# Forget-gate decode of batches 0 to 3 inside chunk compression, one tile per step

## The chip, the cores and the metric

The kernel runs on one core of a Trainium2 chip. The number is the device time of one execution in microseconds (us). Engines are named as in the profile: PE is TensorE's matmul, PEld its weight load, DVE is VectorE, ACT is ScalarE, POOL is GpSimd and SP is SyncE; the last two, and sometimes ACT, issue transfers. They run their own programs and meet at semaphores.

## What is computed

One layer of a hybrid decoder for a prompt of 256 tokens and for 8 decoding sequences ("batches") of 4 tokens each, over a paged cache of 2048 rows per sequence. Two mixers run side by side. NSA has 8 query heads over 2 key heads and three branches: attention over compressed blocks, over 16 selected blocks, over a window. FoX (the forget-gate mixer) has 8 heads and full softmax attention, with sums of log forget gates added to the logits. A gated merge and a convolutional FFN follow. Cut to what the change touches:

```python
def compress_rows(rows, pe, w1, b1, w2):            # once for keys, once for values
    chunks = rows.reshape(B, nc, 16, 2, 64)
    lo = einsum('bcpgd,pdh->bcgh', chunks + pe[:16], w1[:16])
    hi = einsum('bcpgd,pdh->bcgh', chunks + pe[16:], w1[16:])
    return einsum('bcgh,he->bcge', gelu(lo[:, :-1] + hi[:, 1:] + b1), w2)

def fox_attend(q, cq, segs):                        # segs: the cache, then the new rows
    logits = [einsum('bthd,bshd->bhts', q, k) * scale + cq - ck for k, v, ck in segs]
    pr = masked_softmax(concat(logits))
    return sum(einsum('bhts,bshd->bthd', pr_part, v) ...)
```

The FoX cache is 4 MB of keys and 4 MB of values per sequence, 64 MB in all; the compressed NSA caches are 16 MB, the selected ones 16 MB.

## The kernel before

The program is a row of stages (tokens, projection, prompt attention, compression, decode, merge, FFN), each a block in which every engine has its own list of instructions in an order written by hand. Two stages matter.

**Compression** (`stage_compress`, from line 1028; 177.4 to 337.8 in the profile). Sixteen tiles of 1 MB (8 for keys, 8 for values) are gathered into four raw buffers by POOL (`gather`, L1006). The work has `NSTEP` = 32 steps; four steps make a group of two tiles, four groups the keys and four the values. In step k, `fill` (L1143) turns an eighth of two raw tiles by 8 PE transposes into two PSUM banks; pairs of banks alternate, 0 and 1, 2 and 3, and a fill runs two steps ahead. `evacuate` copies the banks to a rounded high part on ACT (L246) and the rest to a low part on DVE (L251). `hidden` (L1166) takes 48 products of these with the high and low parts of the first-layer weights `w1`, in banks 4 and 5. Those parts are made a quarter at a time by `weights` (ACT, then DVE) in steps 0 to 3 for the keys and in steps 12 to 15 for the values. `gelu` (L1257) follows each group, `outputs` a step later through bank 6, and bank 7 serves the norm of the compressed keys and the prompt's attention over chunks. The raw `w1` of the values is loaded in one go (SP, L1014) over that of the keys, once these are split (`w_low` at 4).

**Decode** (`stage_decode`, 337.8 to 577.2). Tiles of 1 MB come through a ring of `DEC_RING` = 8 buffers, gathered by POOL (L1461) as each buffer is freed, 84 in all. Batches 0 to 3 are half 0, batches 4 to 7 half 1. A half of FoX has 16 key tiles: `turn_keys` (L1627) makes 16 transposes into four banks of four, ACT (L1874) and DVE (L1855) copy them out by turns, `key_products` (L1738) takes 4 products of 512 columns into bank 4; every fourth tile adds the forget bias (L1736) and is taken by DVE (L1955). ACT takes the exponentials (L1880), PE turns the probabilities (L1636). Then 16 value tiles (`fox_values`, L1806), 4 products each; after four of them DVE copies the sums out of bank 6 (`take_slots`, L2072) and PE folds them (L1811) in bank 7. NSA of the same half runs between: scores, a selection by DVE in six parts (`select`), its key and value tiles, a merge. `decode_steps` is the hand-written list of all these steps, and `decode_order` puts the turning of one step ahead of the products of the one before; PE, ACT and DVE all walk this one list, each in its order. At the end of the stage the gate weights of the merge are split and multiplied (`split`, `gates`).

## Time and profile before

| | |
|---|---|
| time, median of 3 runs | 930.11 us (929.46 to 933.62) |
| span of the profiled execution | 930.0 us |
| PE busy | 864.0 us, 93% |
| DVE, ACT, POOL busy | 513.4, 378.5, 160.9 us |
| DMA | 191.89 MB, mean 206 GB/s |

The span runs from the first to the last instruction of the profiled execution, and that execution has no time of its own in the results; its span lies 0.1 us from the median of the runs, so that next to nothing lies around it. Busy time of an engine is the time in which at least one of its instructions was running. A matmul's record includes the way through the array, so records overlap; the pace of a run of them is read from the starts, and a busy PE isn't one at its peak. "Idle before" is the time in which an engine had nothing before an instruction, with what ended it. PEclk is the granted clock of TensorE as a share of 2.4 GHz.

### The profile page before, as it was taken

To read this page: it belongs to the slowest core of one execution; us is meant where nothing else is said; L and a number is where in the kernel's file an instruction comes from. 1 tells how busy PE (TensorE), PEld (TensorE's weight loads), DVE (VectorE), ACT (ScalarE), POOL (GpSimd) and SP (SyncE) were. 2 spreads that over 40 slices of the span, in tenths; PEclk is the share of its full clock that TensorE was granted. 3 is DMA by queue.
4 is the path that set the end of the run, shared out by engine and by line. 5 is a ranking of instruction groups with operands and counts; after the bars stand their busy time and mean duration, and the time that the engine had idled before them with its cause. 6 is when DMAs were issued, how large, how long until landed. Compare 5 with 4: busy or idle time off the path is not lost. (4 is left out here: it accounts for less than half of the span.)

```text
span 930.0 us, 18007 instructions
## 1 busy us (share of the span) xinstructions
PE 864.0 (93%) x7191; PEld 708.9 (76%) x7191; DVE 513.4 (55%) x941; ACT 378.5 (41%) x704; POOL 160.9 (17%) x262
## 2 busy tenths in 40 slices
PE   4999788799999999999998977999979999999997
PEld 3888678689889977655655455998679998998985
DVE  5466567433434566754367434465656565565654
ACT  4346575542424323453224422443244443444432
POOL 2000041211121022333434511000001010010100
PEclk8999989999999899999999999999979999999999
DMA  6542195164424269989999994966054544555412
GB/s 218 164 162 87 25 319 221 56 156 136 162 94 182 92 262 385 327 325 418 418 416 420 382 409 121 297 216 223 9 175 149 175 136 135 165 199 177 135 45 61
DMA packets 90640, 191.89 MB, mean 206 GB/s; under 512 B 7466, under 2 KB 68682, under 8 KB 78186
## 3 DMA queue, kind: packets, MB, share of 16 engines
q0 software_dynamic: 15408, 106.04, 29.5%
q1 hardware_dynamic: 74876, 83.91, 29.1%
q8 instruction: 49, 0.80, 0.4%
q10 hardware_dynamic: 288, 0.97, 0.3%
q14 instruction: 19, 0.16, 0.0%
HBM read 187.44 MB, written 7.64 MB: 210 GB/s over the span
## 5 line engine op out<-in xcount | busy, mean ns | idle before, releaser
L1627 PEld LDWEIGHTS banks<-consts_base,stream_rows 128*128 128x128 f32 x672 | 73.4, 142 | 32.7 <-issue 27.3
L1874 ACT ACTIVATE keys_turned<-banks 128x512 f32<-128x512 f32 x94 | 54.9, 596 | 102.1 <-PE banks L1627 97.3
L258 PE MATMUL banks<-tokens_turned_high,w_gates_high 128*128 128x288 f32 x288 | 86.4, 300 | 3.5 <-PEq L191 2.3
L1627 PE MATMUL banks<-consts_base,stream_rows 128*128 128x128 f32 x672 | 83.1, 276 | 6.2 <-DVE fox_probs_turned L1865 2.6
L259 PE MATMUL banks<-tokens_turned_low,w_gates_high 128*128 128x288 f32 x288 | 85.4, 297 | 0.0
L1166 PE MATMUL banks<-chunks_turned_high,cmp_w_high 64*128 64x256 f32 (+1 forms) x512 | 79.6, 303 | 5.3 <-DVE cmp_w_low L251 2.7
L260 PE MATMUL banks<-tokens_turned_high,w_gates_low 128*128 128x288 f32 x272 | 81.7, 300 | 0.0
L1166 PE MATMUL banks<-chunks_turned_low,cmp_w_high 64*128 64x256 f32 (+1 forms) x512 | 76.3, 290 | 0.0
L1166 PE MATMUL banks<-chunks_turned_high,cmp_w_low 64*128 64x256 f32 (+1 forms) x512 | 76.3, 289 | 0.0
L251 DVE TENSOR_TENSOR chunks_turned_low<-banks,chunks_turned_high 128x512 fp32r<-128x512 f32 x64 | 41.1, 684 | 48.0 <-ACT chunks_turned_high L246 48.0
L1855 DVE COPY keys_turned<-banks 128x512 f32<-128x512 f32 x74 | 50.2, 690 | 28.1 <-PE banks L1627 23.1
L246 ACT ACTIVATE chunks_turned_high<-banks 128x512 fp32r<-128x512 f32 x64 | 34.7, 595 | 74.6 <-PE banks L1143 74.6
L1166 PEld LDWEIGHTS banks<-chunks_turned_high,cmp_w_high 64*128 64x128 f32 x512 | 51.9, 194 | 12.7 <-issue 9.3
L258 PEld LDWEIGHTS banks<-tokens_turned_high,w_gates_high 128*128 128x128 f32 x288 | 55.2, 192 | 6.0 <-issue 3.5
L258 PE MATMUL banks<-tokens_turned_high,w_up_gate_high 128*128 128x288 f32 x192 | 58.0, 302 | 0.0
L260 PE MATMUL banks<-tokens_turned_high,w_up_gate_low 128*128 128x288 f32 x192 | 57.1, 297 | 0.0
L259 PE MATMUL banks<-tokens_turned_low,w_up_gate_high 128*128 128x288 f32 x192 | 56.7, 295 | 0.0
L259 PEld LDWEIGHTS banks<-tokens_turned_low,w_gates_high 128*128 128x128 f32 x288 | 55.6, 193 | 0.4
L1166 PEld LDWEIGHTS banks<-chunks_turned_high,cmp_w_low 64*128 64x128 f32 x512 | 52.4, 194 | 0.1
L1166 PEld LDWEIGHTS banks<-chunks_turned_low,cmp_w_high 64*128 64x128 f32 x512 | 52.1, 194 | 0.0
L260 PEld LDWEIGHTS banks<-tokens_turned_high,w_gates_low 128*128 128x128 f32 x272 | 52.0, 191 | 0.0
L2692 POOL COPY conv_new_state<-up_turned 128x2 f32 (+1 forms) x24 | 16.4, 681 | 200.4 <-ACT up_turned L2658 200.4
(451 smaller groups left out, 2107.0 us busy)
## 6 DMA issues: line engine op xcount, KB each, us to landing
w_up_gate<-in_w_up SPq DMA_DIRECT2D x12, 1024.0 KB, 7.3
w_up_gate<-in_w_gate SPq DMA_DIRECT2D x12, 1024.0 KB, 9.8
w_down<-in_w_down SPq DMA_DIRECT2D x12, 1024.0 KB, 5.1
w_in_slot<-in_w_in SPq DMA_DIRECT2D x7, 1424.0 KB, 6.2
w_gates<-in_w_in SPq DMA_DIRECT2D x10, 512.0 KB, 7.3
cmp_w<-in_cmp_w_k SPq DMA_DIRECT2D x4, 512.0 KB
cmp_w<-in_cmp_w_v SPq DMA_DIRECT2D x4, 512.0 KB
stream_rows<-in_state_win_k SPq DMA_DIRECT2D x8, 256.0 KB
```

What stands on the lines that cost most here:

```text
L246: return nc.scalar.activation(high, x, ACT.Copy)
L251: return nc.vector.tensor_tensor(low, x, high.bitcast(F32), ALU.subtract)
L258: nc.tensor.matmul(out, lh, rh, start=start, stop=False, **kw)
L259: nc.tensor.matmul(out, lh, rl, start=False, stop=False, **kw)
L260: return nc.tensor.matmul(out, ll, rh, start=False, stop=stop, **kw)
L1166: ins = nc.tensor.matmul(c.ps[4 + g][:, 0:w], x[rows, half * CS + 4 * q + i, :], y[k % 2][rows, i, src], start=(q + i + half + part == 0), ...
L1627: ins = nc.tensor.transpose(bank(t)[:, q * P:(q + 1) * P], src, ident)
L1855: copy(kT[kbuf[step]][:, x, :], bank(t)).then_inc(copied[e], 1)
L1874: copy = lambda a, b: nc.scalar.activation(a, b, ACT.Copy)
L2692: nc.gpsimd.tensor_copy(dst[:, :, 0:2], ue[f][:, SEQ:SEQ + 2].unsqueeze(1))
```

## The change

FoX of half 0 leaves decode and is done in compression. Steps 0 to 15 take one key tile each (`key_at`), steps 18 to 30 one value tile, two in steps 20, 23 and 26 (`value_at`); steps 16 and 17 turn the probabilities. Two new buffers take the tiles by turns (`gather_fox`): one in the region where the low weights stood, one beside the raw weights. For that, the low parts of `w1` are written over the raw ones (`cmp_w1_low` at the address of `cmp_w1`), the raw value weights come in quarters, each after the last use of its keys' quarter (`load_w1_late`), and they are split in steps 14 to 17. PSUM banks 2 and 3 go to the new work, so fills have only banks 0 and 1 and run one step ahead; bank 7 sums the new logits and values, and what used bank 7 uses bank 2. `hidden` is called in two halves with the turning of two blocks of a key tile before each. The sums of log forget gates move from decode to steps 1 to 3. Decode keeps NSA of both halves and FoX of half 1, in a new order. The turned prompt keys stand apart from the sample's (`kT_prompt`, `fkT_prompt`), so that their place can be used for the turned key tiles. `outputs` of the FoX rows of half 0 are made at the end of compression.

The core of the diff:

```diff
             for m in range(NB):
                 pool.wait_ge(qk, m + 1)
                 chunks.gather(m)
+            chunks.gather_fox(0)
...
+    def load_w1_late(self, sp, q):
+
+        for g in range(NG):
+            for half in range(2):
+                rows = slice(half * CS + 4 * q, half * CS + 4 * q + 4)
+                sp.dma_start(self.w1[g * HD:(g + 1) * HD, rows, :], self.c.d["cmp_w1_v"][0].rearrange("s e h -> e s h")[:, rows, :]).then_inc(self.load_late[q], 16)
...
+    key_at = {k: k for k in range(NU)}
+    early = (20, 23, 26)
+    value_at, n = {}, 0
+    for k in range(NU + 2, NSTEP - 1):
+        m = 2 if k in early else 1
+        value_at[k] = tuple(range(n, n + m))
+        n += m
...
-        bank = lambda k, x: c.ps[2 * (k % 2) + x]
+        bank = lambda k, x: c.ps[x]
+        copied_probs = {1: (1, 33), 2: (0, 33), 3: (1, 34), 4: (0, 34), 0: (0, 35)}
+        bank_of_probs = {1: 3, 2: 2, 3: 3, 4: 2, 0: 7}
         @block.sync
         def _(sp):
+            c.load_fox(sp)
             load_consts(sp)
-            c.load_fox(sp)
-            sp.wait_ge(w_low, 4)
-            chunks.load_w1(sp, 1)
+            for q in range(4):
+                sp.wait_ge(used, 4 * (NGR - 1) + q + 1)
+                chunks.load_w1_late(sp, q)
...
+            def fox_rows(n):
+                if n < NU + 2:
+                    pool.wait_ge(f_turned, 4 * (n - 2) + 4)
+                else:
+                    pool.wait_ge(f_values, n - 2 - NU + 1)
+                chunks.gather_fox(n)
...
+            def turn_keys(u, x):
+                t = 4 * u + x
+                if x == 0:
+                    pe.wait_ge(chunks.fox_in[u % 2], 16 * (u // 2 + 1))
+                if t >= 2:
+                    pe.wait_ge(f_copied[x % 2], t // 2)
+                for q in range(4):
+                    ins = nc.tensor.transpose(c.ps[2 + x % 2][:, q * P:(q + 1) * P], tiles[u % 2][:, q, x * P:(x + 1) * P], c.k("ident"))
+                ins.then_inc(f_turned, 1)
...
+            def new_values():
+                pe.wait_ge(f_copied[0], copied_probs[0][1])
+                pe.wait_ge(f_copied[1], copied_probs[3][1])
...
             fill(0)
-            fill(1)
             for k in range(NSTEP):
                 G, q = divmod(k, 4)
-                hidden(k)
-                if k + 2 < NSTEP:
-                    fill(k + 2)
+                values_now, unit = value_at.get(k, ()), key_at.get(k)
+                if k + 1 < NSTEP:
+                    fill(k + 1)
+                if unit is not None:
+                    turn_keys(unit, 0)
+                    turn_keys(unit, 1)
+                if k == 4:
+                    new_keys()
+                if k == NU + 2:
+                    new_values()
+                if values_now:
+                    values(values_now[0])
+                hidden(k, 0)
+                if unit is not None:
+                    turn_keys(unit, 2)
+                    turn_keys(unit, 3)
+                if values_now and values_now[0] % 4 == 3:
+                    fold_slots(values_now[0] // 4)
+                hidden(k, 1)
+                if unit is not None:
+                    key_products(unit)
+                if k == 1:
+                    logf_sums()
+                if k == NU:
+                    turn_probs(1)
+                    turn_probs(2)
+                if k == NU + 1:
+                    turn_probs(3)
+                    turn_probs(4)
+                    turn_probs(0)
...
+                for i in values_now[1:]:
+                    values(i)
+                    if i % 4 == 3:
+                        fold_slots(i // 4)
...
             outputs(NT - 1)
+            pe.wait_ge(f_out, 1)
+            for q in range(4):
+                ins = nc.tensor.transpose(c.ps[7][:, q * P:(q + 1) * P], fo[:, q * P:(q + 1) * P], c.k("ident"))
...  (ACT, in step k)
                 if k + 1 < NSTEP:
                     evacuate(k + 1)
+                if unit is not None:
+                    fox_keys(unit, 1)
+                if k == NU:
+                    soften(1)
+                    soften(2)
+                if k == NU + 1:
+                    fox_probs(1, 1)
+                    soften(3)
+                    soften(4)
+                    soften(0)
+                if k == NU + 2:
+                    fox_probs(3, 3)
                 if G == 0 and q < 3:
                     weights(0, q + 1)
-                if G == NGR - 1:
-                    weights(1, q)
+                if 0 <= k - (4 * NGR - 2) < 4:
+                    weights(1, k - (4 * NGR - 2))
+                if unit is not None:
+                    fox_keys(unit, 3)
...  (DVE, in step k)
+                if unit is not None:
+                    fox_keys(unit, 0)
                 if k + 1 < NSTEP:
                     evacuate(k + 1)
+                if k == 2:
+                    logf_rows()
+                if k == 3:
+                    cum_rows()
+                if 0 <= k - (4 * NGR - 2) < 4:
+                    weights(1, k - (4 * NGR - 2))
+                if unit is not None:
+                    fox_keys(unit, 2)
+                if k == NU + 1:
+                    fox_probs(2, 2)
+                if k == NU + 2:
+                    fox_probs(4, 4)
+                    fox_probs(0, 5)
...  (the order of decode, new)
+    start = (fox(1, 0) + [("sums", "both", 0, 0)] + fox(1, 1, 2) + rows + fox(1, 3, 4) + new("nsa", 0) + new("fox", 1) + fox(1, 5) + exps("cmp", 0, 0)
+             + fox(1, 6) + norm(0) + fox(1, 7) + score(0) + fox(1, 8) + select(0, 0) + fox(1, 9) + select(0, 1) + nsa(0, 0) + select(0, 2) + fox(1, 10)
+             + select(0, 3) + exps("win", 0, 0) + select(0, 4) + fox(1, 11) + select(0, 5) + fox(1, 12) + nsa(0, 1, 2) + fox(1, 13) + nsa(0, 3) + fox(1, 14)
+             + nsa(0, 4) + fox(1, 15) + nsa_probs(0, 0, 1) + exps("sel", 0, 0, 1) + nsa_probs(0, 2) + exps("fox", 1, 1, 2) + exps("sel", 0, 2, 3, 4)
+             + exps("fox", 1, 3, 4, 0) + nsa_probs(0, 3, 4))
+    middle = (probs(1, 1, 2) + nsa_probs(0, 5, 6) + probs(1, 3, 4) + vals(1, 0) + nsa_probs(0, 7) + probs(1, 0) + vals(1, 1) + nsa_vals(0, 0) + vals(1, 2) + nsa_vals(0, 1)
+              + vals(1, 3) + nsa_vals(0, 2) + fold("fox", 1, 0) + vals(1, 4) + nsa_vals(0, 3) + vals(1, 5) + fold("nsa", 0, 0) + merge("nsa", 0) + vals(1, 6) + new("nsa", 1)
+              + out("nsa", 0) + vals(1, 7) + exps("cmp", 1, 0) + fold("fox", 1, 1) + norm(1) + vals(1, 8) + score(1) + select(1, 0) + vals(1, 9) + select(1, 1) + nsa(1, 0)
+              + select(1, 2) + vals(1, 10) + select(1, 3) + exps("win", 1, 0) + select(1, 4) + vals(1, 11) + select(1, 5) + fold("fox", 1, 2))
+    end = (nsa(1, 1, 2, 3) + vals(1, 12) + nsa(1, 4) + nsa_probs(1, 0, 1) + vals(1, 13) + exps("sel", 1, 0, 1, 2) + nsa_probs(1, 2) + exps("sel", 1, 3, 4)
+           + nsa_probs(1, 3, 4, 5, 6, 7) + branch(0) + vals(1, 14) + nsa_vals(1, 0) + branch(1)
+           + split(0) + branch(2) + nsa_vals(1, 1) + branch(3) + vals(1, 15) + nsa_vals(1, 2) + gates(0, 0) + nsa_vals(1, 3) + fold("nsa", 1, 0) + fold("fox", 1, 3) + merge("nsa", 1)
+           + merge("fox", 1) + gates(0, 1) + out("nsa", 1) + split(1) + out("fox", 1) + gates(1, 0) + split(2) + gates(1, 1))
```

## Rows read from the trace of the kernel before

**Rows 1.** The page, its first part: busy us of each engine and instructions.
```profile
PE 864.0 (93%) x7191; PEld 708.9 (76%) x7191; DVE 513.4 (55%) x941; ACT 378.5 (41%) x704; POOL 160.9 (17%) x262
```

**Rows 2.** Busy time by window: compression, decode, and the middle of decode.
```profile
core 0: us, PE busy (x) PEld busy (x) DVE busy (x) ACT busy (x) POOL busy (x), PEclk, DMA share, GB/s
177.40:337.80 160.40, 153.44 (x1888) 140.11 (x1889) 70.50 (x118) 56.69 (x95) 25.46 (x41) 0.96 0.43 140
337.80:577.20 239.40, 220.34 (x2080) 140.50 (x2081) 130.74 (x281) 86.54 (x164) 78.54 (x81) 0.99 0.93 364
...
420.00:560.00 140.00, 127.09 (x1290) 78.20 (x1286) 68.06 (x146) 45.12 (x88) 51.14 (x53) 0.98 1.01 409
```

**Rows 3.** PE's timeline in decode: start, us, engine, line, operation, count.
```profile
361.41 1.97 PE L1627 MATMUL banks<-consts_base,stream_rows 128*128 128x128 f32 x16
363.31 1.07 PE L1738 MATMUL banks<-keys_turned,fox_q_decode 128*32 128x512 f32 x8
364.31 1.97 PE L1627 MATMUL banks<-consts_base,stream_rows 128*128 128x128 f32 x16
...
419.13 1.06 PE L1806 MATMUL banks<-stream_rows,fox_probs_turned 128*32 128x512 f32 x8
420.02 1.04 PE L1738 MATMUL banks<-keys_turned,fox_q_decode 128*32 128x512 f32 x8
```

**Rows 4.** PE's timeline, waits: in brackets the idle time before, and its releaser.
```profile
203.38 0.39 PE L1166 MATMUL banks<-chunks_turned_high,cmp_w_high 64*128 64x256 f32 x2 [1.47 <-ACT cmp_hidden L1257]
...
505.56 1.09 PE L1627 MATMUL banks<-consts_base,stream_rows 128*128 128x128 f32 x4 [2.29 <-DVE fox_probs_turned L1865]
...
540.57 0.27 PE L1772 MATMUL banks<-sample_rows_kept,nsa_probs_turned 128*32 128x128 f32 x1 [2.12 <-DMA stream_rows<-in_cache_sel_v,eighth_row]
...
543.05 1.06 PE L1806 MATMUL banks<-stream_rows,fox_probs_turned 128*32 128x512 f32 x8 [0.65 <-DMA stream_rows<-in_cache_fox_v,fox_row]
546.52 0.35 PE L1772 MATMUL banks<-sample_rows_kept,nsa_probs_turned 128*32 128x128 f32 x1 [2.40 <-DMA stream_rows<-in_cache_sel_v,eighth_row]
```

**Rows 5.** PE's timeline in a compression step: the fill, the first products, the next fill.
```profile
206.45 1.09 PE L1143 MATMUL banks<-consts_base,stream_rows 128*128 128x128 f32 x8
207.47 0.39 PE L1166 MATMUL banks<-chunks_turned_high,cmp_w_high 64*128 64x256 f32 x2
...
210.54 1.09 PE L1143 MATMUL banks<-consts_base,stream_rows 128*128 128x128 f32 x8
```

**Rows 6.** Groups by line, ACT in compression: count | busy us, mean ns | idle before.
```profile
L246 ACT ACTIVATE chunks_turned_high<-banks 128x512 fp32r<-128x512 f32 x64 | 34.7, 595 | 74.6 <-PE banks L1143 74.6
L246 ACT ACTIVATE cmp_w_high<-cmp_w 128x1024 fp32r<-128x1024 f32 x8 | 8.5, 1061 | 9.0 <-PE banks L1166 9.0
...
L1257 ACT ACT_TABLE_LOAD x3 | 3.8, 1283 | 2.4 <-DVE cmp_bias L1330 2.4
```

**Rows 7.** Groups by line, DVE in compression.
```profile
L251 DVE TENSOR_TENSOR chunks_turned_low<-banks,chunks_turned_high 128x512 fp32r<-128x512 f32 x64 | 41.1, 684 | 48.0 <-ACT chunks_turned_high L246 48.0
L251 DVE TENSOR_TENSOR cmp_w_low<-cmp_w,cmp_w_high 128x1024 fp32r<-128x1024 f32 x8 | 9.8, 1225 | 8.3 <-ACT cmp_w_high L246 7.8
```

**Rows 8.** Timeline of DVE and ACT in decode.
```profile
471.81 1.46 DVE L2087 COPY nsa_sample_out_turned<-banks 64x16 f32<-64x16 f32 x8
...
487.21 1.09 DVE L1997 TENSOR_TENSOR block_compared<-block_scores 128x900 f32<-128x900 f32 x1
...
496.26 0.71 ACT L1880 ACTIVATE fox_logits<-fox_logits,fox_negmax 128x512 f32<-128x512 f32 x1
...
539.33 2.29 DVE L251 TENSOR_TENSOR w_gates_low_early<-w_gates_early,w_gates_high_early 128x2048 fp32r<-128x2048 f32 x1 [1.11 <-ACT w_gates_high_early L246]
```

**Rows 9.** DMA issues from 186 to 340: count, median us from issue to landing.
```profile
stream_rows<-in_cache_cmp_v,eighth_row POOLq DMA_INDIRECT x8, 8.4
```

**Rows 10.** Busy time by window, columns as in rows 2: two stretches at a lower clock.
```profile
506.00:509.00 3.00, 3.00 (x16) 1.50 (x18) 0.98 (x5) 0.60 (x1) 2.08 (x3) 0.50 1.02 426
...
182.00:188.00 6.00, 5.94 (x49) 5.72 (x50) 2.13 (x3) 0.46 (x1) 0.02 (x1) 0.50 0.01 3
```

**Rows 11.** POOL's timeline: the gather of an nsa value tile.
```profile
525.03 1.01 POOL L1461 DMA_INDIRECT stream_rows<-in_cache_sel_v,eighth_row  x1 [0.30 <-issue]
```

457 lines of the change are left out of this document (309 added, 148 removed).

## Prediction

> **What bounds the kernel now.** I read the totals first [rows 1]: PE is busy for 93% of the span, 66 us are left, and that is all that a rearrangement of equal work can win. Then the windows by stage [rows 2]. Chunk compression (177.4 to 337.8) has 6.96 us without a matmul (160.40 - 153.44) at 140 GB/s; decode (337.8 to 577.2) has 19.06 us (239.40 - 220.34) at 364 GB/s, and from 420 to 560 it moves 409 GB/s with the DMA share at 1.01. So the reader sees two claims to the bound in decode, PE and DMA. The third view, PE's timeline, says which ends last: a forget-gate key tile is 16 transposes and 4 products that start at 361.41, 363.31 and 364.31, 2.90 us one behind the other without a gap, and a value tile takes 0.89 us (419.13 to 420.02) [rows 3]. A pair of tiles is 3.8 us of PE for 2.1 MB, 552 GB/s: above what the DMA gives, but the keys alone want only 362. Of decode's 19.06 us of idle PE, a transfer ended 5.17 (2.12 + 0.65 + 2.40) [rows 4]; the rest waited for a DVE or ACT that was busy elsewhere, as in the 2.29 us before 505.56, or lay in short gaps. The DMA is full, yet mostly behind PE. What bounds is PE, in its program order.
>
> **The work that moves.** 16 key tiles and 16 value tiles leave decode: 16 x 2.90 + 16 x 0.89 = 60.6 us, and with the bias products, the folds, the new keys and values and the turned probabilities (none changed in number or shape) some 74 us. The same instructions are added to compression, so this term is zero in the sum, whatever its size, as long as PE's pace is the same in both places.
>
> **Compression, what is new on PE.** A step of it is now one fill of 8 transposes, 1.02 us (206.45 to 207.47), and 48 products of `hidden`, 3.07 us (to 210.54) [rows 5]. The change cuts `hidden` in two with transposes between. The first pair of a run costs more than the steady pace: the 24 pairs at 0.12 us would be 2.86, so a run has 0.21 us at its ends, 16 more of them: **+3.4 us**. A key step then lasts 1.0 + 0.95 + 1.64 + 0.95 + 1.64 + 1.0, about 7.1 us. I laid each engine's queue beside it, with 0.60 us for a 128x512 copy on ACT and 0.68 on DVE, and 1.06 (ACT) and 1.23 (DVE) for a quarter of the weights [rows 6, 7]. In most key steps everything is ready: `evacuate` ends at 3.6, the last key copies at 4.7 (DVE) and 5.1 (ACT), the products want them at 5.9. The single pair of fill banks costs nothing then, because the fill is asked for a whole step later. The cover fails in five places:
> - Step 2: DVE has `logf_rows` (three operations of 128x512 or its like, 1.9 by the row of 0.68), then a weight quarter, then the third key copy, at 7.5 instead of 6.4: **1.1**.
> - Step 16: two exponentials (0.71 each [rows 8]) come behind a table load of 1.28 [rows 6]: **0.4**.
> - Step 17: ACT does evacuate, a probability copy, three exponentials and only then the last quarter of the v weights (ends 5.7); DVE waits for that, splits it (6.9), and copies piece 2 (7.6). PE has stood before the turn of piece 4, which needs that bank, since 4.7: **3.0**.
> - Step 18: `new_values` stands behind only a fill, but wants pieces 4 and 0, which DVE copies after `evacuate(19)`: ready at 4.1, wanted at 1.0: **3.1**.
> - Steps 20, 23, 26: the second value tile of the step is followed at once by its fold, which waits for a 0.68 copy and two semaphores: 3 x 0.95 = **2.9**.
>
> At the end DVE has the merge (0.6 + 0.75) and four sums more behind the last product: **1.5**. Given back: the two waits for the hidden rows (1.47 at 203.38 [rows 4] and its like in the other half, 1.1), since key work now lies before them: **-2.6**. Sum of the stalls 9.4 us. ACT's queue otherwise has room. POOL's: each gather costs it about 1.0 and stands behind the tail of the next group, which waits for `used`; it is still two steps ahead. SP's: the v weights are issued by quarters as `hidden` frees them, 10 us before ACT wants them. For a gather in compression the nearest row is 8.4 us to landing for two issued together [rows 9]; the window from release to use is 2 x 5.1 - 1 = 9.2 us in value steps and 10 in key steps. I take nothing for it.
>
> **Decode.** Its 19.06 us of idle fall by the 5.17 of transfers: 32 of 84 ring tiles are gone, so 54.5 MB remain, 133 us at 409 GB/s, against about 145 us of PE. But the same keys that left were the cover for the selection of the other half. In the new order:
> - End of `start`: ACT has ten exponentials in a row (6 us and more) before it copies turned piece 3 of the nsa probabilities, whose bank piece 5 wants: **3.4**, where before key tiles lay between.
> - `new`, `out` (eight copies, 1.46 us), `take_slots`, then a fold with one value tile (0.89) as cover: **2.9**. Then three steps of `select` (1.09 each), a window maximum and the slot copy before the next fold: **3.7**. Waiting for the nsa merge: **0.5** [rows 8].
> - `end`: the split of gate weights (2.29 on DVE, after ACT's half of it [rows 8]) stands before the slot copy that nsa_vals(1,2) needs: **3.0**. `out` nsa and the next split before gates(1,0), with half a microsecond of PE as cover: **3.7**. Smaller: **1.3**.
> - Kept: 0.7 in the keys, 2.3 at the stage's end.
>
> Together 21.5, **+2.4** against 19.06.
>
> **The clock.** After the 2.29 us without a matmul at 503 the granted clock was 0.50 for 506 to 509, and at the first `hidden`, which waits for its weights, it was 0.50 for 182 to 188 [rows 10]: the lower of its two levels, 1.2 GHz. An episode of 3.4 to 6.8 us by those rows costs half of that in PE work. The two stages have waits of 2.3 us or more about five times now and I count nine after. Four more at 1.7 would be 7; as PE at half pace also shortens the waits behind it, I take **+4**. Bounds: 0 (the waits break up) and +13.
>
> **A rule that speaks the other way.** The row first: in decode LDWEIGHTS are busy 140.50 of 239.40 us, 59%, under a DMA share of 0.93 [rows 2]. The Trainium skill, Perfetto Trace Analysis, "Identifying the Most-Contended Engine", says that matmul busy time is no measure of how near PE is to its limit and that LDWEIGHTS and the DMA are to be compared; its "Optimization Strategy" advises mixing stages with different limits, and that is this change. By it decode would shrink with its bytes and compression would swallow the tiles. I go by the gapless timeline [rows 3] for the forecast, and give the rule its own case.
>
> **The sum.** 930.0 (the span; the median of the runs is 930.11, so both stand for each other) + 3.4 + 9.4 + 2.4 + 4 = **949**.
>
> **Rivals.**
> - *Relief of the DMA.* The mechanism in this kernel: most idle of decode is really late data in small portions, and it goes with the bytes. 930 - 13 (two thirds of 19.06) - 2.6 + 3.4 + half of the new waits in compression (6) = **924**. For it: 1.01 share for 140 us. Against: only 5.17 us have a transfer as releaser.
> - *A draw.* The waits of DVE's order overlap each other more than I reckon, so half of the 12 and half of the 21.5 appear: 930 + 3.4 + 3.4 + (11 - 19) + 2 = **932**.
> - *The gathers become the wait.* Two buffers instead of eight. With the ring full a tile was issued at 525.03 and its value products began at 540.57 [rows 4, 11], 15.5 us; if, beside the 512 KB quarters and the chunk pairs, one takes 2 us more than its window in eight steps, that is 16 us: **965**. It decides from a landing of 9.2 us after release.
>
> **How the numbers follow.** Forecast 0.60, relief 0.15, draw 0.12, gathers 0.13. The forecast's own range, from clock at 0 and stalls at two thirds to clock at +13, is 940 to 960. The range reaches to the draw and to the gathers, 928 to 965. About 0.5%, 4.6 us, is what a measurement of this kernel can tell from no change. Faster: the relief, 0.15. Same: the draw, 0.12. Slower: the forecast and the gathers, 0.73.
>
> **What would show it.** Right: compression 240 to 260 us long, with PE idle before the turn of piece 4 and before `new_values` and released by DVE; decode 165 to 175 us, no PE wait ended by a transfer, its waits ended by slot copies and splits; more stretches at 0.50. Wrong: decode under 155 us (relief), or key steps in compression with PE waiting for `fox_rows_early` (gathers), or a key step far from 7.1 us, which would mean that PE's pace isn't the same there.

## The result, and the profile after

The changed kernel takes 975.71 us (median of 4 runs, 972.41 to 978.46), the kernel before 929.79 beside it: a ratio of 1.051, 95% interval 1.0473 to 1.0547, **45.9 us slower**. The forecast was 949, 19 us slower, with a range up to 965. The direction was right, the size was not, and the time lies outside the range.

The totals, and the two stages by window (columns as in rows 2):

```profile
PE 880.1 (91%) x7191; PEld 713.9 (74%) x7191; DVE 513.2 (53%) x941; ACT 380.0 (39%) x706; POOL 159.6 (16%) x262
```

```profile
core 0: us, PE busy (x) PEld busy (x) DVE busy (x) ACT busy (x) POOL busy (x), PEclk, DMA share, GB/s
178.60:442.05 263.45, 239.86 (x2511) 183.60 (x2511) 105.71 (x191) 81.44 (x141) 53.60 (x72) 0.94 0.60 209
442.05:618.70 176.65, 150.06 (x1457) 102.12 (x1458) 95.51 (x208) 63.17 (x120) 48.44 (x49) 0.95 0.81 303
540.00:560.00 20.00, 13.09 (x101) 6.31 (x93) 11.73 (x31) 2.71 (x5) 6.60 (x7) 0.91 1.02 395
```

The same 7191 matmuls are busy 16.1 us longer than before [rows 1]. The two stages lasted 160.40 + 239.40 = 399.8 us [rows 2] and last 263.45 + 176.65 = 440.1: all of the 40.4 us between the two spans lies in them (the stages ahead are 1.2 longer, those behind 1.1 shorter). Idle PE in them was 6.96 + 19.06 = 26.0 and is 23.6 + 26.6 = 50.2, 24.2 more; the other 16.1 are matmuls that take longer. So there are two accounts to settle, where PE waits and why its work is slower; the forecast had 11.8 for the first (9.4 + 2.4) and 7.4 for the second (3.4 + 4).

The difference of the medians is 5.5 us more than that of the two spans. 3.3 of it is that the profiled execution of the changed kernel (972.41) is the fastest of its four. The rest lies on the side of before: its span of 930.0 is 2 us longer than goes with its median of 929.79, as 1.7 to 2.4 us lie outside the span in the executions whose time and span are both on record. (The record doesn't say which time belongs to that span; the first listed, 933.62, is likely.) Part of this is the clock: the four executions of the changed kernel have a mean granted clock of 0.964, 0.959, 0.955 and 0.960, the profiled one the highest, and that of before has 0.972, where all executions of before beside the experiments, on other chips, have 0.973 to 0.987. So what the spans below give to the clock is rather too little for the medians.

Where PE waits in compression: its timeline, with the idle time and its releaser in brackets.

```profile
322.49 0.63 PE L1326 MATMUL banks<-consts_fox,fox_logits_early 128*128 128x128 f32 x4 [3.48 <-DVE fox_logits_early L1577]
...
329.74 1.90 PE L1336 MATMUL banks<-sample_rows_kept,fox_new_logits_early 128*32 128x512 f32 x8 [2.87 <-DVE fox_new_logits_early L1577]
...
371.37 1.93 PE L1348 MATMUL banks<-fox_rows_early,fox_logits_early 128*32 128x512 f32 x8 [2.75 <-DMA fox_rows_early<-in_cache_fox_v,fox_row]
...
432.36 0.66 PE L1425 MATMUL banks<-consts_base,fox_rows_out_early 128*128 128x128 f32 x4 [0.39 <-DVE fox_rows_out_early L1590]
442.09 3.22 PE L1953 MATMUL banks<-consts_base,stream_rows 128*128 128x128 f32 x14 [9.07 <-PEq L191]
```

The first two are the turn of piece 4 and `new_values`, as forecast. The third is a tile that came late. The fourth line is PE's last work of the stage and the fifth the first of decode: 9.07 us with the barrier (L191) as releaser, where before there were 1.66:

```profile
337.81 1.94 PE L1627 MATMUL banks<-consts_base,stream_rows 128*128 128x128 f32 x16 [1.66 <-PEq L191]
```

DVE's last sums began at 433.39 and took 1.27; behind them nobody computes. POOL had this:

```profile
430.16 0.94 POOL L1790 DMA_INDIRECT stream_rows<-in_cache_fox_k,fox_row  x1 [7.30 <-PE banks L1244]
431.40 0.93 POOL L1790 DMA_INDIRECT stream_rows<-in_cache_fox_k,fox_row  x1 [0.30 <-issue]
442.71 0.93 POOL L1790 DMA_INDIRECT stream_rows<-in_cache_fox_k,fox_row  x1 [10.38 <-POOLq L191]
```

Ring tiles 4 and 5 are gathered last, behind the final product of `hidden` (the change made them wait for `used` at its end, as their place is freed then), and the barrier's drains (L191) stand at 441.3, 9.0 us behind the last gather. Ahead of them every engine has a drain of its own at the end of its list (L188), and POOL's is long: first in the changed kernel, then in the kernel before, with ns of duration and the start.

```profile
L188 POOLq DRAIN  x1: 11151/11151/11151, 429.9 to 429.9; - x1
...
L188 POOLq DRAIN  x1: 9994/9994/9994, 326.0 to 326.0; - x1
```

It ends at 441.1, 2.0 us behind the landing of the last gather (7.6 us after its issue at 431.40). In before it ended at 336.0, 8.5 us behind the last gather of the stage (issued at 327.51) and 0.9 us ahead of DVE's.

And in decode:

```profile
520.60 1.65 PE L1979 MATMUL banks<-consts_base,sel_logits 128*128 128x128 f32 x8 [2.66 <-ACT nsa_probs_turned L2191]
...
546.39 0.62 PE L2130 MATMUL banks<-fox_slot_sums,consts_base 128*32 128x512 f32 x1 [2.90 <-DVE fox_slot_sums L2368]
...
552.36 3.28 PE L1953 MATMUL banks<-consts_base,stream_rows 128*128 128x128 f32 x16 [2.39 <-DMA stream_rows<-in_state_win_k]
...
562.36 1.92 PE L2130 MATMUL banks<-fox_slot_sums,consts_base 128*32 128x512 f32 x2 [3.02 <-DVE fox_slot_sums L2368]
...
593.67 0.27 PE L2093 MATMUL banks<-sample_rows_kept,nsa_probs_turned 128*32 128x128 f32 x1 [2.58 <-DVE nsa_slot_sums L2339]
...
608.68 0.40 PE L264 MATMUL banks<-tokens_turned_high,w_gates_high 128*128 128x288 f32 x1 [3.45 <-DVE w_gates_low_in_place L257]
```

Five of the six were forecast by name, with sizes up to 0.7 us above these. The third was not: window keys that landed late, in a stretch where the DMA share is 1.02 at 395 GB/s and PE is busy for 13.09 of 20 us (the last window above).

### The profile page after: what moved, and what is told of

Its sections match the earlier page's. It is cut to its first block and busy times, and to the rows that moved or that the text cites. A ratio compares the mean times of both kernels' runs of the same rounds, so it can differ in the third digit from the quotient of the medians.

```text
span 970.4 us, 18010 instructions
## 1 busy us (share of the span) xinstructions
PE 880.1 (91%) x7191; PEld 713.9 (74%) x7191; DVE 513.2 (53%) x941; ACT 380.0 (39%) x706; POOL 159.6 (16%) x262
## 5 line engine op out<-in xcount | busy, mean ns | idle before, releaser
L1244 PE MATMUL banks<-chunks_turned_low,cmp_w_high 64*128 64x256 f32 (+1 forms) x512 | 73.8, 283 | 0.0
L1244 PE MATMUL banks<-chunks_turned_high,cmp_w_low 64*128 64x256 f32 (+1 forms) x512 | 73.7, 283 | 0.0
L1953 PEld LDWEIGHTS banks<-consts_base,stream_rows 128*128 128x128 f32 x416 | 48.6, 148 | 32.0 <-issue 28.7
L1953 PE MATMUL banks<-consts_base,stream_rows 128*128 128x128 f32 x416 | 54.3, 287 | 13.2 <-PEq L191 9.1
L1244 PEld LDWEIGHTS banks<-chunks_turned_high,cmp_w_high 64*128 64x128 f32 x512 | 49.3, 188 | 19.9 <-issue 17.3
L2191 ACT ACTIVATE keys_turned<-banks 128x512 f32<-128x512 f32 x62 | 35.8, 596 | 68.1 <-PE banks L1953 68.0
L1244 PEld LDWEIGHTS banks<-chunks_turned_low,cmp_w_high 64*128 64x128 f32 x512 | 49.5, 189 | 0.0
L1244 PEld LDWEIGHTS banks<-chunks_turned_high,cmp_w_low 64*128 64x128 f32 x512 | 49.3, 188 | 0.0
L1524 DVE COPY fox_keys_early<-banks 128x512 f32<-128x512 f32 x32 | 22.1, 690 | 46.3 <-PE banks L1292 43.0
```

The source lines that it names most:

```text
L1244: ins = nc.tensor.matmul(c.ps[4 + g][:, 0:w], wt[rows, half * CS + 4 * q + i, :], y[k % 2][rows, i, src], start=(q + i + half + part == 0) ...
L1524: nc.vector.tensor_copy(kq[x][:, :], c.ps[2][:, :]).then_inc(f_copied[0], 1)
L1953: ins = nc.tensor.transpose(bank(t)[:, q * P:(q + 1) * P], src, ident)
L2191: copy = lambda a, b: nc.scalar.activation(a, b, ACT.Copy)
```

## Experiments

Each kernel was timed beside the kernel before on its chip, which gave 926.6 to 927.8 us there; the changed kernel at its ratio of 1.051 would be about 975 beside it. Differences under about 5 us between two changed kernels are inside the intervals. Stage lengths and waits are those of one profiled execution each.

**Late gathers out of compression (e1).** Two gathers cross a stage boundary:

```
-            for n in range(6):
-                if n < 4:
-                    pool.wait_ge(turned, NSTEP - 4 if n < 2 else NSTEP)
-                else:
-                    pool.wait_ge(used, NSTEP)
+            for n in range(4):
+                pool.wait_ge(turned, NSTEP - 4 if n < 2 else NSTEP)
                 gather_decode_rows(c, n)
...
-            for n in range(6, len(ring)):
+            for n in range(4, len(ring)):
```

> The changed kernel, but the gathers of ring tiles 4 and 5, which stood behind the last product of hidden at the end of compression, are POOL's first two of decode instead. In the changed kernel PE stood still for 9.07 us before decode, and every engine's drain lay 8.9 us behind POOL's last gather (431.40 + 0.94 to 441.3). Theory A (the stage can't end until POOL's last gathers have landed): that wait falls to the 1 to 2 us of before, the 10.2 us at half clock behind it is gone too, decode's later tiles come no later; 975.7 - 7.4 - 1.8 = about 966, between 963 and 969. Theory B (the boundary waits for something else, DVE's sums or the barrier itself): time within 2 us of 975.7 and the wait still about 9 us. If tiles 4 and 5 come too late for PE in decode, a wait ended by a transfer of stream_rows shows before 460 and gives back 2 to 5 us.

Measured: 967.27 us, ratio 1.0432 (1.0391 to 1.0472), 7.2 us of the 9.2 expected. The first rows of decode, on PE and on POOL:

```profile
433.17 3.39 PE L1950 MATMUL banks<-consts_base,stream_rows 128*128 128x128 f32 x16 [2.91 <-PEq L191]
```

```profile
419.16 0.94 POOL L1787 DMA_INDIRECT stream_rows<-in_cache_fox_k,fox_row  x1 [0.30 <-issue]
433.79 0.94 POOL L1787 DMA_INDIRECT stream_rows<-in_cache_fox_k,fox_row  x1 [13.69 <-POOLq L191]
```

The wait fell from 9.07 to 2.91, and no tile came late at decode's start (later there are 5.7 us of waits for data, against 3.2). So the two late gathers held the stage open (theory A). POOL's own drain now ends at 428.9, again 2.0 us behind the landing of its last gather (426.9), and that is no longer last: the barrier's drains at 432.4 stand behind DVE's four sums (430.64 + 1.27 and their latency). The 2.91 us are the 1.66 of before and 1.25 more, near the 1.5 for the stage's end which the forecast had.

```profile
L188 POOLq DRAIN  x1: 11202/11202/11202, 417.7 to 417.7; - x1
```

**DVE's and ACT's order (e2).** The copies of the turned probabilities first, and a fold that followed its value tile at once moved into the next step:

```
+                if k == NU + 1:
+                    fox_probs(2, 2)
+                if k == NU + 2:
+                    fox_probs(4, 4)
+                    fox_probs(0, 5)
                 if k + 1 < NSTEP:
                     evacuate(k + 1)
...
+                while late:
+                    fold_slots(late.pop())
                 hidden(k, 1)
...
                     values(i)
                     if i % 4 == 3:
-                        fold_slots(i // 4)
+                        late.append(i // 4)
```

> The changed kernel with two orders mended: in steps 17 and 18 DVE and ACT copy the turned probabilities first, ahead of the evacuation and the weight quarter; and the three folds that followed their value tile at once are done in the middle of the next step. In the changed kernel PE waited 3.48 us before the turn of piece 4, 2.87 before new_values and 0.81 + 0.80 + 0.81 before those folds, 8.8 together. Theory A (a wait of over about 2.4 us also costs a stretch at half clock behind it, 3.4 us long at 322.9 and at 329.7 in the profiled run): 8.8 - 0.5 that stays, and 3.4 for the clock, so 975.7 - 11.7 = about 964, between 962 and 967. Theory B (only the waits go): 975.7 - 8.3 = 967.4. Theory C (the waits of DVE are made up elsewhere in the same steps): less than 4 us, over 971.5.

Measured: 964.93, ratio 1.0398 (1.0353 to 1.0444), 10 us less: theory A by the forecast and by the trace, though the interval holds B's 967.4 too. The wait of 3.48 and the three of 0.8 are gone, 1.67 is left before `new_values`, and the granted clock is 1.00 from 322 to 352 where it was 0.72 from 322 to 334.

**Value gathers ahead of chunk gathers (e3).** POOL's order within a step:

```
-                if q == 2 and G + 2 < NT:
-                    pool.wait_ge(turned, 4 * G + 4)
-                    for b in range(2):
-                        chunks.gather(2 * (G + 2) + b)
                 for i in value_at.get(k, ()):
                     if i + 2 < NU:
                         fox_rows(NU + i + 2)
+                if q == 2 and G + 2 < NT:
+                    pool.wait_ge(turned, 4 * G + 4)
+                    for b in range(2):
+                        chunks.gather(2 * (G + 2) + b)
```

> The changed kernel with POOL's order in each third step of a group turned: the gathers of the forget-gate rows stand ahead of the two gathers of chunk rows, which nobody wants for five steps. In the changed kernel the value tile used at 371.37 was issued at 361.60, behind the chunk gathers of 359.12 and 360.36, and PE waited 2.75 us for it; 6.8 us at half clock followed. Theory A (the two chunk gathers, 2.1 MB, lie in front of it on the same queue): the wait is gone and with it the stretch at half clock, 975.7 - 2.75 - 3.4 = 969.5, between 968 and 973. Theory B (a landing simply takes longer than a step's window there): the wait stays within 1 us, time within 2 us of 975.7.

Measured: 971.54, ratio 1.0476 (1.044 to 1.0512), about 3 us less, inside what can't be told apart. The trace tells more: the tile at 371 came in time, and another was late instead, behind the same pair of chunk gathers:

```profile
363.14 0.93 POOL L1018 DMA_INDIRECT stream_rows<-in_cache_cmp_v,eighth_row  x1 [0.30 <-issue]
365.75 0.93 POOL L1027 DMA_INDIRECT fox_rows_early<-in_cache_fox_v,fox_row  x1 [1.68 <-PE banks L1348]
```

```profile
375.25 1.60 PE L1348 MATMUL banks<-fox_rows_early,fox_logits_early 128*32 128x512 f32 x8 [2.23 <-DMA fox_rows_early<-in_cache_fox_v,fox_row]
```

From 365.75 to 375.25 are 9.5 us. The rival of late gathers had put the line at 9.2. A tile of the same size with nothing in front of it landed 5.5 us after its issue (350.17, the same run).

**Quarter rows in compression (e7).** It leaves out three quarters of the rows of the forget-gate tiles gathered there:

```
+        w = P // 4 if n >= 2 else P
-        nc.gpsimd.indirect_dma_start(self.fox[n % 2][:, :], None, table, ...
+        nc.gpsimd.indirect_dma_start(self.fox[n % 2][0:w, :], None, table, ...
```

> The changed kernel, but the forget-gate gathers inside compression move 32 of 128 rows each (from the third on): 23 MB less in compression, the same instructions otherwise; what the other rows hold is left from the first tiles. It measures everything that gathering into two buffers costs there. Theory A (PE bounds compression, one gather of 32 comes late): the wait of 2.75 us at 371.37 and the 6.8 us at half clock behind it go, 975.7 - 6 = about 969.5, between 968 and 973. Theory B (the rival of the forecast: gathers are late in eight steps and more): 960 or less. Theory C (the DMA's load slows what else uses memory, so PE's pace in key steps falls with the bytes): key steps of 7.9 to 8.6 us become shorter by 0.3 or more.

Measured: 972.12, ratio 1.0489 (1.0445 to 1.0532). B is out: all the bytes of these tiles together are worth 2 us, 6 at most. But A had the wrong cause, as its wait stayed:

```profile
368.87 1.07 PE L1349 MATMUL banks<-fox_rows_early,fox_logits_early 128*32 128x512 f32 x8 [2.38 <-DMA fox_rows_early<-in_cache_fox_v,fox_row]
```

A tile of 0.26 MB, issued at 359.51, was as late as one of 1 MB. What it had in front of it was the pair of chunk gathers, unchanged (356.99 and 358.26). C is out too: all key steps behind the first last as long as in the changed kernel, to 0.01 us (8.06, 7.88, 8.45 and so on in both).

**The three together (e5).** e1, e2 and e3 in one kernel.

> The changed kernel with the three mendings together: late gathers moved into decode, DVE's and ACT's order in steps 17 and 18 with the folds in the next step, value gathers ahead of chunk gathers. Alone they gave 7.6, 10 and 3.4 us against the changed kernel at 1.051 times the kernel before. Theory A (they lie in different places and add up): ratio 1.051 - 0.0225 = 1.028, between 1.025 and 1.032, which is 26 us over the kernel before, and what the forecast left out is explained. Theory B (tiles that are asked for sooner meet a full DMA, and waits for transfers take the place of the others): 1.034 to 1.040, with more than 5 us of PE waits ended by transfers in the view of the waits.

Measured: 960.83, ratio 1.0359 (1.0317 to 1.0401): 14 us, not the 21 of the parts. That is theory B's range, though with four intervals in the comparison the 7 us are not clear of them. PE came sooner to a tile that had the pair in front of it:

```profile
353.44 0.93 POOL L1018 DMA_INDIRECT stream_rows<-in_cache_cmp_v,eighth_row  x1 [0.30 <-issue]
356.05 0.94 POOL L1027 DMA_INDIRECT fox_rows_early<-in_cache_fox_v,fox_row  x1 [1.68 <-PE banks L1345]
```

```profile
366.08 1.94 PE L1345 MATMUL banks<-fox_rows_early,fox_logits_early 128*32 128x512 f32 x8 [4.62 <-DMA fox_rows_early<-in_cache_fox_v,fox_row]
```

The waits ended by a transfer sum to 8.4 us in its two stages, 5.9 in the changed kernel; so theory B's sign of more than 5 us didn't tell the two apart. The stages tell more. Compression fell by 15.7 us (263.5 to 247.8), against 8.1, 10.5 and 3.5 in e1, e2 and e3, 22 together. Waits for value tiles there are 6.5 us against 2.7, which is 3.8 of the 6.4 that are missing: that much is theory B. Decode is 4.1 us longer (180.8 against 176.7) at the same idle PE (25.7 and 26.6), because its granted clock was 0.92 and not 0.95; in e1, e2 and e3 it lasted 179.5 to 179.9 at 0.92 to 0.93. What moves the clock there from one execution to the next isn't settled.

**The pair taken apart (e9).** e1 and e2, one chunk gather in each of two steps, behind the value gather, and two value tiles in steps 20, 24 and 28:

```
-    early = (20, 23, 26)
+    early = (20, 24, 28)
...
+                if q >= 2 and G + 2 < NT:
+                    pool.wait_ge(turned, 4 * G + 4)
+                    chunks.gather(2 * (G + 2) + q - 2)
```

> The mendings of e1 and e2 together, and the gathers of compression spread: the two gathers of chunk rows, which POOL issued one behind the other, in two steps, each behind the value gather of its step, and the steps with two value tiles moved from 20, 23, 26 to 20, 24, 28. In e5 a value tile issued at 356.05, behind the chunk pair of 352.20 and 353.44, ended a wait of 4.62 us at 366.08; with quarter rows (e7) the wait at that place was still 2.38 us, so it is the pair of 1 MB gathers in front of a tile, not the tiles' own bytes. Theory A (the pair in front is the cause): no PE wait over 1 us ended by fox_rows_early, no stretch at half clock at 365 to 373, so 960.8 - 4.6 - 1.6 - 3.4 = about 951, ratio 1.024 to 1.031 to the kernel before. Theory B (two buffers are too few however the gathers stand): waits of 3 us and more in all remain somewhere from 340 to 420 and the ratio is 1.033 or more.

Measured: 955.38, ratio 1.0275 (1.0234 to 1.0316), theory A in the main: PE's waits for these tiles in compression fell to

```profile
PE banks L1344 <- DMA fox_rows_early<-in_cache_fox_v,fox_row: 2.0, 2, 1.4
```

(total, count, longest), the longest still over the 1 us expected, and the stretch of 6.8 us at half clock there is 3.4 (at 371.7), though the expectation had none left. In decode, though, waits for transfers grew to 7.1 us: `fox_rows` 6.4 and window keys 0.7, against 3.2 in the changed kernel. That this comes of what was mended upstream is not shown: the same waits were 6.7 us in e3, whose decode and boundary are those of the changed kernel, and 1.9 in e5.

**Bytes taken out of decode of before (e4).** It leaves out three quarters of the rows of the forget-gate tiles of batches 0 to 3 there:

```
+    w = P // 4 if job == "fox" and half == 0 and n >= DEC_RING else P
-    c.nc.gpsimd.indirect_dma_start(c.stream[r][:, :], None, table, ...
+    c.nc.gpsimd.indirect_dma_start(c.stream[r][0:w, :], None, table, ...
```

> The kernel before, unchanged in order, but the gathers of the forget-gate tiles of batches 0 to 3 in decode (from the ninth ring tile on) move only 32 of 128 rows: about 19 MB less in decode; what the other rows hold is left from earlier tiles. It tells the largest gain that taking these bytes out of decode could bring. Theory A (PE bounds decode, the DMA is full behind it; the view of the forecast): only the waits that a transfer ended in the first half may go, and those of 540.57, 543.05 and 546.52 lie in the second half: 929.8 - 0 to 3, so 927 to 930. Theory B (the rival: two thirds of decode's 19 us of idle PE is late data): 929.8 - 8 to 13, so 917 to 922.

Measured: 925.33, ratio 0.9978 (0.9955 to 1.0): 2 us, 4 at most. In its profiled execution decode lasted 235.0 us against 239.4 (1.7 of these 4.4 are the clock), and transfers ended 4.2 us of waits against 5.17, with the DMA share down from 0.93 to 0.83. Theory A; the relief that rows 2 seem to offer (a share of 1.01 for 140 us) is not there to be had. The expectation calls it the largest gain, but it leaves out 19 MB of the 33.6 that the change moves, none from the first eight ring tiles.

**One value tile moved in decode (e8).**

```
-              ... + vals(1, 6) + new("nsa", 1)
-              + out("nsa", 0) + vals(1, 7) + exps("cmp", 1, 0) ...
+              ... + vals(1, 6) + vals(1, 7) + new("nsa", 1)
+              + out("nsa", 0) + exps("cmp", 1, 0) ...
```

> The changed kernel with one step of decode moved: the value tile vals(1,7) stands ahead of new(nsa,1) and out(nsa,0), so that DVE's slot copy of batch 5 comes ahead of the eight copies of out (1.46 us) and PE has new and out as cover before fold(1,1). In the changed kernel that fold waited 2.90 us at 546.39. Theory A (DVE's order is the cause, as the forecast has it): the wait falls under 1 us, with half of a 3.4 us stretch at half clock: 975.7 - 2.5 - 1.7 = about 971.5, between 970 and 973.5. Theory B (the DMA is full there, 395 GB/s from 540 to 560 at a share of 1.02, and PE only waits for the next tile instead): the wait for the fold goes and waits ended by stream_rows grow by as much; time within 2 us of 975.7.

Measured: 972.32, ratio 1.0485 (1.0446 to 1.0524): between the two theories, and inside what can't be told apart from no gain. The trace decides: the wait for the fold is gone, so DVE's order was its cause, and two others stand in its place, one for a tile and one for DVE again.

```profile
541.50 1.94 PE L2125 MATMUL banks<-stream_rows,fox_probs_turned 128*32 128x512 f32 x8 [1.69 <-DMA stream_rows<-in_cache_fox_v,fox_row]
550.00 0.46 PE L2043 MATMUL banks<-cmp_logits,consts_select 128*128 128x128 f32 x2 [2.53 <-DVE cmp_logits L2284]
```

1.69 + 2.53 is more than the 2.90 that went, while the 2.39 for the window keys fell to 0.36. So the wait for the fold was mended and others came; waits for data in decode were 2.5 us in all, against 3.2.

**PE kept busy in three waits (e6).** `spin(bank, n)` is n transposes of the identity into a free bank, which nobody reads:

```
+                    spin(6, 26)
                     turn_probs(4)
...
+                    spin(6, 20)
                     new_values()
...
             ins.then_inc(f_out_turned, 1)
+            spin(1, 68)
```

> The changed kernel with useless transposes of a constant on PE ahead of three of its waits: 26 before the turn of piece 4 (3.48 us), 20 before new_values (2.87), 68 before the end of compression (9.07), none of them longer than the wait that it fills, so the waits for DVE and for the drain end when they did. Theory A (the clock falls because PE stood still): the stretches at half clock that began at 322.9, 329.7 and 435.5 are gone, PE's work behind them takes 1.7 + 1.7 + 1.8 = 5.2 us less: about 970.5 against 975.7, and the granted clock of 322 to 334 and of 440 to 446 is 1.00. Theory B (it falls for the load of the whole chip or by a rhythm of its own): the same stretches at half clock, somewhere near, and a time within 2 us of 975.7.

Measured: 967.84, ratio 1.043 (1.0382 to 1.0478), 7 us less. The same stretches in both kernels, first the changed one (the column after POOL's count is the granted clock):

```profile
322.00:334.00 12.00, 8.63 (x45) 5.02 (x47) 2.92 (x7) 1.57 (x3) 2.28 (x3) 0.72 0.43 153
...
442.00:446.00 4.00, 3.91 (x20) 3.94 (x21) 1.47 (x3) 0.82 (x2) 1.86 (x2) 0.51 0.76 275
```

```profile
322.00:334.00 12.00, 10.87 (x112) 8.68 (x110) 3.73 (x8) 1.58 (x3) 4.76 (x4) 1.00 0.51 176
...
440.00:446.00 6.00, 6.00 (x53) 5.00 (x54) 3.48 (x7) 2.39 (x4) 3.62 (x4) 1.00 0.84 304
```

The three waits were ended by the same events (DVE's copies and POOL's drain don't depend on the fillers), and the three stretches at 0.50, the lower level of 1.2 GHz, are gone. So it was PE's standing still that they followed from, not a rhythm of the chip. In the changed kernel's two stages these stretches cost 23.8 us of PE work by the granted clock of each microsecond (3.3 of it inside the 9.07 us wait, where nothing was lost), against 10.2 in before: **+10.3**. (The short idle times inside the other stretches are still in it; by busy PE alone the difference is 9.5.)

**Fillers in the kernel before (e10, e12).** If the clock is worth that much, before should gain too.

```
+            spin(nc, c, 6, 17)
...
+            pe.wait_ge(z_out[1], NZC)
+            spin(nc, c, 4, 20)
...
+                    if n == 2:
+                        spin(nc, c, 6, 24)
...
+            spin(nc, c, 2, 12)
...
+                    spin(nc, c, 7, 21)
...
+            spin(nc, c, 7, 20)
...
+            spin(nc, c, 0, 24)
...
+            spin(nc, c, 0, 14)
```

> The kernel before with useless transposes of a constant on PE in eight of its waits, nothing else changed: 17, 20 (behind a wait for ACT's last copy of the bank that they write) and 12 at the ends of the first three stages, 24 and 21 ahead of the first wait of attention and of compression, 20 at the end of decode, 24 and 14 at the end of the merge; 0.12 us each, about as long as the waits or shorter. In the profiled run of before, half clock followed these waits at 17 to 25, 113 to 124, 181 to 189, 577 to 581 and 679 to 690, 18.7 us of PE time lost in all. Theory A (the clock falls because PE stood still, as e6 showed in the changed kernel): most of these stretches go, and the time falls by 8 to 17 us, to a ratio of 0.982 to 0.991. Theory B (the chip takes the clock back elsewhere, or the waits were what the clock needed): stretches at half clock appear in other places, ratio 0.996 to 1.003. If a filler outlasts its wait, up to 0.5 us is lost in each place.

Measured: 924.03, ratio 0.9962 (0.9944 to 0.998): a gain, but 3.5 us instead of 8 to 17. The first filler ran at half the pace and outlasted its wait:

```profile
15.34 3.89 PE L372 MATMUL banks<-consts_base 128*128 128x128 f32 x17
20.00 1.40 PE L515 MATMUL banks<-w_in_slot,sample_turned 128*32 128x356 f32 x16 [0.77 <-PEq L191]
```

That is 0.23 us each, where the 68 of e6 took 7.59 us, 0.11 each. The half is read from the pace alone: the column of the granted clock shows 1.00 there, and its first record in this run stands at 19.6. So it was left out, and the others fitted better (e12, against e10):

```
-            spin(nc, c, 6, 17)
...
-            spin(nc, c, 2, 12)
+            spin(nc, c, 2, 7)
...
+                    if step == ("keys", "nsa", 1, 1) and x == 3:
+                        pe.wait_ge(fox_taken, 10)
+                        spin(nc, c, 4, 17)
                     free_bank(t)
```

> The kernel before with the fillers of e10 where they fit: none at the end of the first stage (there they ran at half clock, took 4 us instead of 2 and moved the second stage's first product from 16.99 to 20.00), 7 instead of 12 at the end of attention, and 17 more in decode before the fourth bank of nsa key tile 1 of the second half, where PE waited 2.29 us. Theory A (fillers keep the clock and cost nothing inside a wait): e10's 924.0 less 3 for the first place, 0.6 for the third and 1.7 for the new one: about 919, ratio 0.988 to 0.994. Theory B (what a filler gives back in clock is lost again in the next wait, as PE then only reaches it sooner): ratio 0.994 to 0.998, as e10.

Measured: 923.64, ratio 0.9967 (0.995 to 0.9985). Theory B in its size, but not for its reason: the clock did stay up, at 0.992 for the profiled execution against 0.972, and the stretches came back in one place only (6.8 us at 535.6, around a wait of 3.43 for data, where before had 3.4 us at 546.6). What is wrong is the price: half clock took 26.2 us from PE's full speed in the profiled execution of before and 7.4 in this one, and the spans differ by 7.3. In attention the granted clock rose from 0.92 (110 to 177.4, with half clock from 113 to 124) to 1.00, 5.1 us of PE work by the count above, and the stage became 0.6 us shorter (112.18 to 177.41 before, 112.83 to 177.44 now), because ACT's exponentials bound its beginning and not PE: the products that wait for them begin 5.26 us into the stage in both (117.44 and 118.09). In compression, where PE is the bound, 4.1 of 5.1 us came through, in a window that begins with the first fill in both:

```profile
177.40:333.70 156.30, 151.57 (x1910) 138.34 (x1910) 70.50 (x118) 56.70 (x95) 25.49 (x41) 0.99 0.45 144
```

156.3 against 160.4 us [rows 2]. **This kernel and e10 are the fastest here**, a third of a per cent below before; between the two (0.9967 and 0.9962) nothing can be told.

**Everything mended (e11).** e9 with the fillers of e10 (but the one in compression) and those in eight more places that the expectation lists (it says six), among them

```
             def fold_slots(half, b):
+                if b in (1, 2):
+                    spin(nc, c, 4, 22)
                 pe.wait_ge(acc_taken, b + 1)
...
                 br = "cmp" if i == 0 else "win" if i < 3 else "sel"
+                if (half, i) == (0, 5):
+                    pe.wait_ge(fox_taken, 5)
+                    spin(nc, c, 4, 20)
```

> e9 and the fillers of e10 in the changed kernel, with six more: 15 before the second fill, 11 before new_values, 22 at the end of compression, 20 before the turn of nsa piece 5, 22 before each of the folds of batches 5 and 6, 20 before the nsa values of batch 6, 27 before the last gate products. Theory A: the changed kernel without its mended waits and with the clock kept: e9's time less 15 to 25 us, ratio 1.000 to 1.012, so the move is worth nothing even with its faults mended: what stays is the split of hidden (3.4 us) and decode's waits for DVE. Theory B (fillers only shift the clock's low stretches): ratio as e9's within 0.004.

Measured: 948.24, ratio 1.0204 (1.0173 to 1.0236), 6.6 us less than e9 by the ratios. Neither theory: fillers give a part of what the count of the clock promised, as in before. The second one shown stood behind the wait that it was to fill (20 matmuls at 502.12, after 2.66 us of idle, and PE's next work at 506.02), which cost 3.9. Even so mended, the move is 2% slower than not moving.

## Why the prediction was wrong, point by point

- **PE is the bound; the moved work costs the same in both places.** Right. Matmuls are equal in number, and a plain key step takes 7.1 to 7.2 us (262.49 to 269.62, 247.16 to 254.34), the forecast's 7.1; steps with bias products or `outputs` beside it take 7.9 to 8.6. e4, with 19 of the 33.6 MB out, gained 2 us where the rival of relief wanted 8 to 13: that rival is out.
- **The split of `hidden`, +3.4.** Right. In the same trace a whole run of 48 products takes 3.07 us (3.25 for 274 columns) and a half 1.63 (1.73, as from 208.42 to 210.15), so a split costs 0.19 to 0.21; with 49 runs where there were 32 that is 3.3 us.
- **The stalls in compression.** Step 17: 3.0 forecast, 3.48 measured; step 18: 3.1 and 2.87; three folds: 2.9 and 2.42; step 2: 1.1 and 0.46; step 16: 0.4 and nothing. The waits for the hidden rows went as forecast, and e2 shows that they were DVE's and ACT's order. This part of the method held, to 0.7 us a place; together these five came out 1.3 us under the forecast's 10.5.
- **"At the end ... 1.5".** This is the step that failed. It made the boundary 1.66 + 1.5 = 3.2 us, and it was 9.07, 5.9 more, with 1.8 us of half clock behind it. The working took DVE's queue to its end and left out POOL's, although the kernel shows the two gathers and their new condition. POOL's drain lasts until its last gather has landed; in before it already ended only 0.9 us ahead of DVE's, 8.5 us behind the last issue, so the row that would have priced it was there. e1 gave 7.2 us back, and left 2.91. Of a queue that is named (POOL) the last entry before a barrier has to be followed too.
- **"I take nothing for it" (the gathers).** Wrong by 2.75 us and the clock behind it. The window of 9.2 us was right, and so was that a landing of 8.4 fits in it; what was missed is that in one step of four 2 MB of chunk rows stand in front on the same queue, which makes it 9.4 to 10.0 from issue to the end of PE's wait (e7, e3, e5, and 9.8 here). The rival of late gathers had the mechanism, but in eight steps; it was one, and as soon as the other waits were mended it grew to 4.62 (e5).
- **Decode, +2.4.** Forecast 21.5 us idle, measured 26.6. By name: 3.4 (2.66), 2.9 (2.90), 3.7 (3.02), 3.0 (2.58), 3.7 (3.45), all waits for ACT or DVE. Beyond the 21.5 are 5.1 us. The claim that no wait would be ended by a transfer failed: 2.39 + 0.56 + 0.20 us, 3.2 of them; 1.9 are other waits, such as 1.78 for DVE at 487.18 where 0.7 was set down for the keys. The sum of bytes against the sum of PE time was right for the stage (share 0.81) and wrong for 540 to 580, where it is 1.02: a value tile is 1 MB for 0.89 us of PE, far over the 405 GB/s that were moved there, whatever the mean is, and before the move key tiles of 2.90 stood between them. That these late tiles come of it is argued and not shown: in e8, with one wait for DVE mended there, waits for data fell from 3.2 to 2.5.
- **The clock, +4.** The mechanism held for three waits and is shown by e6; the size was 10.3, inside the bounds (0 to 13), so the term of 4 was 6.3 too small. Nine waits of 2.3 us or more were counted and ten there are, and there are ten stretches at half clock (four before); but the forecast priced a new one at 3.4 us of half clock, and at the late tile it was 6.8 us, at the boundary 10.2, of which 6.5 lay inside the wait. Wait and stretch are also not one to one: none stands behind the 2.90 us at 546.39 and the 2.58 at 593.67, one follows the 2.01 at 181.69, and one of 6.8 us stands at 384.4 with no wait of 1 us in the ten before it, in before likewise at 300.8. So a count of waits gives the order of the term and not more, and the 2.4 us in the expectation of e2 is no limit.
- **What stays open.** Of the 16.1 us that matmuls took longer, 10.3 are the clock and 3.3 the split; 2.5 have no row of their own. And why e9, with the named faults of compression mended, is still 25 us behind before isn't settled one by one: its two stages last 421.9 us against 399.8: 10.9 of the 22.1 are idle PE (36.9 against 26.0) and 11.2 slower matmuls, 5 of them by the clock and 3.3 by the split.
- **The base.** The forecast set span and median equal, with next to nothing around the span. Every execution whose time and span are both on record has 1.7 to 2.4 us around it, so a sum built on the span of 930.0 forecasts a difference of spans (19 against 40.4) rather than of medians (45.9).
- **The signs and the other sums.** Compression was to last 240 to 260 us and lasts 263.5, decode 165 to 175 and lasts 176.7. The draw's sum as written gives 930.8 and not 932, which changes nothing here.

In one line, span against span: 19.2 forecast, 5.9 more at the boundary, 2.8 for the late tile, 1.5 less for the other stalls of compression, 3.2 for the transfers in decode and 1.9 for its other waits, 6.3 more for the clock and 2.4 unexplained make 40.2 of the 40.4 measured.

## What to carry to other kernels

Work that moves from a stage whose DMA is full to one whose DMA is not brings nothing if PE was the bound in both, and it takes away the cover under which the first stage hid DVE's long operations. Before a barrier, follow every queue to its last entry, the one that only issues transfers above all, and for that one up to the landing of what it issued last. And a window for a transfer holds only for what stands in front of it on its queue: put large gathers that nobody wants yet one at a time behind the one that is wanted next.

## What the runs showed of the hardware

- Around the ends of waits of 2.75, 3.48 and 9.07 us PE's clock was at 1.2 GHz for 6.8, 3.4 and 10.2 us (6.5 of the last inside the wait); useless matmuls in the waits of 3.48, 2.87 and 9.07 kept it at 2.4 (e6). Not every such wait has a stretch (none behind 2.90 and 2.58 us in the changed kernel). Where PE is the bound most of what the clock gives back is gained: 4.1 of 5.1 us in compression (e12). Where ACT is (the beginning of attention) 5.1 us of PE work that the clock gave back shortened the stage by 0.6 (e12).
- Two gathers at the end of a stage held the barrier for 9.0 us behind the last issue, with none of the program's own instructions waiting for their data in the stage (drains at 441.3 after 432.33; 7.2 us less when they were moved, e1). What waits is POOL's own drain: it ended 2.0 us behind the landing of the last gather in both kernels (441.1 after 439.0, and in e1 428.9 after 426.9).
- The landing of a gather behind two others of 1 MB was set by these and not by its own size: a wait for it ended 9.4 us after the issue for 0.26 MB (e7) and 9.5 for 1 MB (e3). With nothing in front, 1 MB landed in 5.5 us (e3, issue at 350.17).
